# Four adaptive modulation units moved from TensorE's matmuls to multiply-and-add passes on VectorE

## What is computed

```python
mod = jax.nn.silu(c) @ w_ada[l] + b_ada[l]            # (1,1024) @ (1024, 6*1024)
shift1, scale1, gate1, shift2, scale2, gate2 = jnp.split(mod, N_MOD, axis=-1)
h  = modulate(rmsnorm(x, norm1_w[l]), shift1, scale1)
...
x  = x + gate1[:, None, :] * mix
h2 = modulate(rmsnorm(x, norm2_w[l]), shift2, scale2)
```

```python
t_mat = lax.linalg.triangular_solve(eye + a_mat, jnp.broadcast_to(eye, a_mat.shape),
                                    left_side=True, lower=True, unit_diagonal=True)
```

## Time and profile before

| | us |
|---|---|
| median of 3 runs (920.33 to 921.24) | 921.1 |
| the profiled execution | 920.74 |
| its span in the profile | 918.9 |
| TensorE busy | 894.8 (97%) |
| VectorE busy | 410.4 (45%) |
| ScalarE busy | 314.3 (34%) |
| GpSimd busy | 106.1 (12%) |

### The profile page before, as it was taken

One profiled execution on the slowest core, in us unless ns is written; L12 is line 12 of the kernel. 1 busy time (PEld: TensorE's weight loads), 2 busy tenths in 40 slices (PEclk: granted clock), 3 DMA queues, 4 the chain that ended last, 5 costly groups with the idle time before them and its releaser, 6 DMA issues.

```text
span 918.9 us, 13421 instructions
## 1 busy us (share of the span) xinstructions
PE 894.8 (97%) x5530; PEld 576.2 (63%) x5530; DVE 410.4 (45%) x697; ACT 314.3 (34%) x507; POOL 106.1 (12%) x116
## 2 busy tenths in 40 slices
PE   5999999999999999999999999999999999999998
PEld 2688876777644434444344444444435899999886
DVE  2457735368522323222222232223233878888744
ACT  1227435243522222232122212222213555555531
POOL 1024463131000000000000000000000022222200
PEclk9999999999999999999999999999999999999999
DMA  9962259787979999999999999999999665545301
GB/s 357 413 289 93 93 194 358 282 331 292 404 275 422 422 420 420 421 421 420 419 421 419 418 421 421 422 420 420 420 421 353 197 190 181 183 184 185 133 1 47
DMA packets 60892, 289.47 MB, mean 315 GB/s; under 512 B 4500, under 2 KB 28692, under 8 KB 33688
## 3 DMA queue, kind: packets, MB, share of 16 engines
q1 hardware_dynamic: 59104, 284.13, 78.0%
q10 hardware_dynamic: 1720, 4.40, 1.2%
HBM read 287.47 MB, written 1.05 MB: 314 GB/s over the span
## 4 chain that ended last, share of the span: by engine, by line
PE 91%; DVE 3%; DMA 2%; issue 2%; ACT 1%; POOL 1%; ACTq 0%; DVEq 0%
PE ps L1031 24%; PE ps L1055 12%; PE ps L536 8%; PE ps L1019 7%; PE ps L1152 7%; PE ps L1153 7%; PE ps L1154 7%; PE ps L619 4%; PE ps L1071 3%; PE ps L551 2%; PE ps L1044 2%; PE ps L519 2%; DMA S<-in_first_cols_dram 1%; DMA ring<-in_ada_units_dram 1%; PE ps L510 1%
## 5 line engine op out<-in xcount | busy, mean ns | idle before, releaser
L1034 PE MATMUL ps<-ring,proj 128*64 128x512 f32 x320 | 140.9, 593 | 0.0
L1031 PE MATMUL ps<-ring,proj 128*64 128x512 f32 x304 | 133.9, 593 | 0.0
L1852 DVE TENSOR_TENSOR w_l<-ring,w_h 128x2048 fp32r<-128x2048 f32 x33 | 75.5, 2291 | 44.8 <-ACT w_h L2200 44.8
L1152 PE MATMUL ps<-h_h,w_h 128*128 128x256 f32 x336 | 95.1, 283 | 0.0
L1153 PE MATMUL ps<-h_l,w_h 128*128 128x256 f32 x336 | 95.1, 283 | 0.0
L1154 PE MATMUL ps<-h_h,w_l 128*128 128x256 f32 x336 | 95.1, 283 | 0.0
L1031 PEld LDWEIGHTS ps<-ring,proj 128*64 128x64 f32 x304 | 41.1, 137 | 84.6 <-issue 84.6
L1708 DVE SCALAR_TENSOR_TENSOR RQ<-ps,gate_of,proj 128x512 f32<-128x512 f32 x32 | 24.0, 750 | 152.3 <-PE ps L1056 152.3
L1031 PE MATMUL ps<-arena,proj 128*64 128x512 f32 x208 | 91.6, 593 | 0.0
L2200 ACT CAST w_h<-ring 128x2048 fp32r<-128x2048 f32 x33 | 62.8, 1902 | 81.4 <-PE ps L1154 76.9
L2156 ACT CAST MX_r<-RQ 64x512 fp32r<-64x512 f32 x62 | 38.2, 616 | 145.8 <-DVE RQ L1708 145.0
(11 more groups left out here) (372 smaller groups left out, 1610.7 us busy)
## 6 DMA issues: line engine op xcount, KB each, us to landing
ring<-in_w_dram SPq DMA_DIRECT2D x114, 1024.0 KB, 16.4
arena<-in_w_dram SPq DMA_DIRECT2D x72, 1024.0 KB, 16.3
ring<-in_ada_units_dram SPq DMA_DIRECT2D x11, 2048.0 KB, 8.5
ring<-in_ffn_w_in_dram SPq DMA_DIRECT2D x22, 1024.0 KB, 7.8
ring<-in_in_units_dram SPq DMA_DIRECT2D x6, 2048.0 KB, 23.0
ring<-in_ffn_w_out_dram SPq DMA_DIRECT2D x5, 2048.0 KB, 8.0
arena<-in_in_units_dram SPq DMA_DIRECT2D x2, 2048.0 KB, 24.7
ring<-in_out_units_dram SPq DMA_DIRECT2D x2, 2048.0 KB, 9.1
```

What stands on the lines that cost most here:

```text
L1031: pe.matmul(ps[0:SLOTS, :], XTe[i % 2][:, k, :], u1[:, k, :], start=(k == 0), stop=(k == 7))
L1034: t = pe.matmul(ps[64:64 + SLOTS, :], XTe[i % 2][:, k, :], u3[:, k, :], start=(k == 0), stop=(k == 7))
L1152: pe.matmul(ps, ah, bh, start=first, stop=False)
L1852: ve.tensor_tensor(low, src, dst.bitcast(F32), ALU.subtract).then_inc(split_ready, 1)
```

## The change

Units 4 to 7 leave TensorE. VectorE makes them from the same loaded weights: a multiply of the first chunk with its column of silu(c) (`ccol`), one scalar for each partition, then seven multiply-and-adds, one for each further chunk, each waiting for the one before it. All 128 partitions now hold a part sum, so the totals multiply with `ones` instead of `sel`. Units 4 and 5 write to `part`, 6 and 7 write to (and read again from) the turned view of `by_eights`. VectorE's list has unit 4 at the end of level 1, unit 5 at the end of level 2, unit 6 in level 3 behind the row totals, unit 7 at the end of level 4. TensorE's `ada(4)` to `ada(7)` and ScalarE's four copies are gone; the row totals 4 and 5 move from level 4 to level 3, behind `project(5)`. The load that takes a unit's place waits for VectorE's last pass (`ada_rows`).

```diff
             def gate_total(j, src):
                 ps = take("total", j)
-                pe.wait_ge(*drained("ada", j))
-                pe.matmul(ps[:, :], sel, src, start=True, stop=True).then_inc(*mm.up("total", j))
+                pe.wait_ge(ada_rows, by_vector.index(j) + 1)
+                pe.matmul(ps[:, :], ones, src, start=True, stop=True).then_inc(*mm.up("total", j))
...
-                elif level == 5:
-                    ada(7)
                 elif level == 2:
                     project(3)
                 elif level == 3:
                     project(5)
-                elif level == 4:
                     gate_total(4, part[0])
                     gate_total(5, part[1])
+                elif level == 4:
                     turn_rotated(0)
...
                 elif level == 2:
                     project(4)
-                    ada(4)
-                elif level == 3:
-                    ada(5)
                 elif level == 4:
                     turn_rotated(1)
-                    ada(6)
...
+            def ada(j):
+
+                w = unit(("ada", j), 512)
+                if j in (4, 5):
+                    ve.wait_ge(*mm.of("columns", 1, 1))
+                    dst, cut = part[j % 2], lambda a: a
+                else:
+                    ve.wait_ge(*mm.of("total", 4))
+                    ve.wait_ge(*mm.of("total", 5))
+                    dst = by_eights[:, :, 64 * (j % 2):64 * (j % 2) + 64].rearrange("k c p -> k p c")
+                    cut = lambda a: a.rearrange("k (p c) -> k p c", c=8)
+                ve.wait_ge(*filled(("ada", j)))
+                ve.tensor_scalar(dst, cut(w[:, 0, :]), ccol[:, 0:1], None, ALU.mult).then_inc(*vd.up())
+                for c in range(1, 8):
+                    ve.wait_ge(*vd.now())
+                    ve.scalar_tensor_tensor(dst, cut(w[:, c, :]), ccol[:, c:c + 1], dst, ALU.mult,
+                                            ALU.add).then_inc(*((ada_rows, 1) if c == 7 else vd.up()))
...
                 if level == 1:
                     lower(3)
+                    ada(4)
                 elif level == 2:
                     lower(5)
+                    ada(5)
                 elif level == 3:
                     gate_total(4)
                     gate_total(5)
+                    ada(6)
+                elif level == 4:
+                    ada(7)
...
                 if kind == "ada":
-                    return mm.of("ada", i)
+                    return (ada_rows, by_vector.index(i) + 1) if i in by_vector else mm.of("ada", i)
```

More of the change, by code:

```diff
@@ L475, in program @@
         chunk_ready_a, chunk_ready_v = sem("chunk_ready_a"), sem("chunk_ready_v")
-        diagonal_ready = sem("diagonal_ready")
+        diagonal_ready, ada_rows = sem("diagonal_ready"), sem("ada_rows")
+        by_vector = (4, 5, 6, 7)
         rows_made, gated, router_scaled, h2_rows = (sem(n) for n in ("rows_made", "gated", "router_scaled", "h2_rows"))
@@ L556, in gate_total @@
                 ps = take("total", j)
-                pe.wait_ge(*drained("ada", j))
-                pe.matmul(ps[:, :], sel, src, start=True, stop=True).then_inc(*mm.up("total", j))
+                pe.wait_ge(ada_rows, by_vector.index(j) + 1)
+                pe.matmul(ps[:, :], ones, src, start=True, stop=True).then_inc(*mm.up("total", j))
             def column_total(seg, half, ps=None):
-                ps = ps or take("columns", seg)
-                pe.wait_ge(*drained("ada", 2 * seg + half))
+                ps, j = ps or take("columns", seg), 2 * seg + half
+                if j in by_vector:
+                    pe.wait_ge(ada_rows, by_vector.index(j) + 1)
+                else:
+                    pe.wait_ge(*drained("ada", j))
                 for c in range(8):
-                    i = pe.matmul(ps[64 * half:64 * half + 64, 2 * c:2 * c + 2],
-                                  by_eights[:, c, 64 * half:64 * half + 64], sel[:, 0:2], start=True, stop=True)
+                    i = pe.matmul(ps[64 * half:64 * half + 64, 2 * c:2 * c + 2], by_eights[:, c, 64 * half:64 * half + 64],
+                                  (ones if j in by_vector else sel)[:, 0:2], start=True, stop=True)
                 i.then_inc(*mm.up("columns", seg, half))
@@ L793, in tensor_program @@
                     ada(10)
-                else:
+                elif level == 6:
                     project(7)
@@ L1909, in ada @@
                 ps, dst = full("ada", j), part[j % 2]
[L1910 to L1914, removed]
+                if j in (8, 9):
+                    ac.wait_ge(*mm.of("columns", 3, 1))
                 elif j > 9:
                     dst = late_part[j % 2]
-                if j in (6, 7, 8, 9):
+                if j in (8, 9):
                     half = slice(64 * (j % 2), 64 * (j % 2) + 64)
```

## The result

The median after is 926.99 us (five runs, 925.49 to 928.67) against 921.1 before (919.5 to 921.66, five runs): a ratio of 1.0067, 95% interval 1.0050 to 1.0084, so 0.67% slower. The profiled execution took 928.67 us, with a span of 926.9; that of before 920.74 and 918.9.

The account below looks back on a forecast made before the run. TensorE, 91% of the chain that ended last, was taken as the bound: 7.4 us taken off, 18.7 put on, mostly waits behind units 6 and 7, so 11.5 us later, 932 us, range 922.5 to 943.

Parts of the forecast that it names:

- TensorE waits for it at the totals: At the level-3 row totals, TensorE would be held until unit 5 ends on VectorE at 135.2: 0.15 us.
- one turned pass: A VectorE multiply-and-add of units 6 and 7, writing and reading its target with a stride: 1.22 us, bounds 0.75 and 2.1.
- price of a collision, for a pass: A VectorE multiply-and-add meeting a GpSimd instruction of 0.72 us would alternate with it and pay about 0.6 us.
- TensorE until level 5 starts: TensorE would wait 11.4 us for the level-4 subtraction, which stands behind unit 6 in VectorE's queue.
- copy of the products, bare: The copy of the level-5 products, formerly hidden by unit 7 on TensorE, would be exposed: 0.7 us.
- wait for a bank before unit 10: TensorE's unit 10 would wait 4.5 us for a bank freed by VectorE's level-5 subtractions, queued behind unit 7.
- wait for the split: In the projection after level 6, TensorE would wait 1.6 us for VectorE's split after its first eight matmuls.
- rival 1: VectorE passes cost 0.78 us whatever the stride and GpSimd doesn't collide: 0.8 us gained, 920.3; chance 0.10.
- Rival 5: TensorE's clock falls in its waits, so sixteen uncovered projection matmuls run at half rate: up to 4 us more, 936; chance 0.12.
- Rival 3: On VectorE, stride paid but GpSimd collisions slight: 4.4 us less than the sum, 928; chance 0.16.
- rival 4: In units 6 and 7, strided reading and writing paid in turn, unit 16 us: twice 6.2 more, 945; chance 0.10.
- point of decision: A unit price of 6.4 us on VectorE decides the sign, since each microsecond of a turned unit counts twice.

Follow-up runs that it names:

- experiment 1: Against the changed kernel, units 6 and 7 went back to TensorE and ScalarE, only 4 and 5 stayed on VectorE: 916.53 us, ratio 0.9945 to before.
- experiment 2: Against the changed kernel, VectorE wrote units 6 and 7 in rows and TensorE took every eighth element when loading weights: 927.09 us, ratio 1.0064 to before.
- experiment 7: Against the changed kernel, GpSimd's eight multiplies that rotate the keys were left out (keys then wrong): 924.89 us, measured once.
- late7: Against the changed kernel, unit 7 moved behind VectorE's level-5 splits, and projection 4 loaded ahead of unit 9: 927.14 us, ratio 1.0060 to before.
- fill: Against the changed kernel, eleven matmuls that nothing reads were put into TensorE's wait ahead of level 5: 929.12 us, ratio 1.0075 to before.
- fill2: Against the changed kernel, unread matmuls in both TensorE waits, eleven ahead of level 5 and five ahead of its scores: 926.44 us, measured once.

## Why the prediction was right in direction and too large in size

Forecast 932.0 with 922.5 to 943, 10.9 over before; measured 927.0, 5.9 over. Slower had 0.90. By its own steps, forecast against measured:

| step | forecast | measured |
|---|---|---|
| unit 4 in rows, GpSimd idle | 6.0 us | 6.0 (0.47 + 5.48 and a step between) |
| unit 5, seven collisions | 10.2, end 135.2 | 9.0, end 133.7 |
| TensorE waits for it at the totals | 0.15 | none |
| one turned pass | 1.22 | 1.11 |
| price of a collision, for a pass | 0.6 | 0.36, plain or turned |
| GpSimd's last rotations start | 139.3 | 137.9 |
| collisions of unit 6 | 7 | 5, and 0.2 on its multiply |
| unit 6 | 14.1 | 10.4 |
| TensorE until level 5 starts | 11.4 | 6.41, and 0.94 for GpSimd's sum |
| copy of the products, bare | 0.7 | 0.94 |
| unit 7 | 9.9 | 8.7 |
| wait for a bank before unit 10 | 4.5 | none; half-rate work, 3.2, in its place |
| wait for the split | 1.6 | 0.67 |
| end of the stretch against before | +11.5 | +5.9 |
| behind it | passed on whole | passed on; 2.3 more in the profiled execution, not in the medians |

**What held.** The mechanism is the forecast one. The low price of units 4 and 5 held (experiment 1), the stride costs (experiment 2), GpSimd costs (experiment 7), level 4 and level 5 wait behind units 6 and 7 in VectorE's queue, and the loads cost nothing (no wait of TensorE for a transfer stands in the stretch). The rule of decision held too: TensorE's waits were to exceed 7.4 us for a slower kernel, and they are 9.4.

**The term that was mis-sized is the price of unit 6.** It was put at 9.9 + 4.2 = 14.1 us; it is 10.4, so 3.7 of the 5.6 that are missing stand there. Of these, 2.4 are the collisions (4.2 against the 1.8 of experiment 7), the rest the passes, which make unit 7 cheaper by the same 1.2. Two slips of the sum hardly matter: rival 1 counts from the median where the sum counts from the profiled execution (0.4 us), and GpSimd doesn't work on until 145 but is idle from 130.6 to 134.9. The collision was priced from one pair of long overlaps as if a pass waited for most of the other's 0.72 us. The line of all passes (duration min/median/max in ns), then one pass of unit 5 and one of unit 6 by themselves, each with the GpSimd instruction that it meets:

```profile
L1258 DVE SCALAR_TENSOR_TENSOR part<-ring,S,part x28: 752/1107/1460, 110.7 to 158.9; 128x512 f32<-128x512 f32 x28
```

```profile
126.83 1.10 DVE L1258 SCALAR_TENSOR_TENSOR part<-ring,S,part 128x512 f32<-128x512 f32 x1
...
141.88 1.46 DVE L1258 SCALAR_TENSOR_TENSOR part<-ring,S,part 128x512 f32<-128x512 f32 x1
```

```profile
126.21 1.18 POOL L2350 TENSOR_TENSOR S<-proj,S 128x256 f32<-128x256 f32 x1
...
137.87 3.05 POOL L2350 TENSOR_TENSOR S<-proj,S 128x256 f32<-128x256 f32 x4
...
141.00 1.43 POOL L2352 TENSOR_TENSOR proj<-S 128x256 f32<-128x256 f32 x1
```

A plain pass is 752 ns and 1.10 in company, a turned one 1107 and 1.46: about 0.36 us each time. The queues do alternate, as forecast (all seven passes of unit 5 take 1.10 to 1.12, the first five of unit 6 1.35 to 1.46), but half of each instruction goes by beside the other. Unit 6 meets only five because the last group of rotations starts at 137.87, not at 139.32 as before: the prediction had it start no earlier, but with unit 4 gone from TensorE the projection that it rotates comes 1.85 us earlier. Three of its four multiplies are over when unit 6 begins at 139.59, which leaves one multiply, two sums and two masks; they end at 146.9. GpSimd pays as well: its multiplies go from about 0.7 (2.78 for four) to 1.18 and its sums to 1.43, which is what TensorE's wait of 0.94 before the level-4 subtraction is for.

The Trainium skill's page SBUF — State Buffer, section Who interferes with whom, has the loser blocked for a whole instruction; here the trace doesn't bear that out for VectorE: by that rule a collision with a 0.72-us instruction would be 0.72, and it costs 0.36. For GpSimd beside a long VectorE instruction the trace agrees: its multiply at 122.71, beside the split that ends at 124.77, takes 2.67 us and ends 0.6 after it.

**The stride.** The pass was put at 1.22 between bounds of 0.75 and 2.1, on the choice that reading and writing don't add. That choice held: 1.11. The same page of the Trainium skill, section Door 1: The DMA port swizzle, lets each step to another 16-byte line pay, without a figure; the trace agrees with the direction, and the figure here is 0.36 us on 512 elements that are read and written so.

**The clock.** Rival 5 had 0 to 4 us, and I took 0: unit 7 on VectorE covers what follows the first wait, and the clock may rise before the projection's last sixteen matmuls. These ran at 1.00 (160 to 170 us in after), but the second wait, which was to lower the clock ahead of them, didn't come. As for the cover, late7 and fill show that the clock and unit 7 cover each other almost exactly, and fill2 that the stretch is no shorter with the clock at 2.4 GHz throughout. But the forecast had TensorE reach the bank early and wait 4.5 us there; it came late and slow instead. That this part of the sum has nearly its forecast size (3.2 + 0.67 against 4.5 + 1.6) is in part luck: the reason is one that it named only as a rival's.

**The chances.** Rival 3 (collisions slight, 928) came nearest in time, by 1 us, in part by luck: it had no collisions and dearer passes, and the two errors offset each other. Rival 1 and rival 4 fell with the first turned unit. The point of decision was given as 6.4 us for a unit. In rows beside GpSimd unit 6 took 7.9, and free of it unit 7 took 6.0; that kernel's stretch was still 2.6 longer than before, so for unit 6 it agrees. No run had both units under 6.4.

## What to carry to other kernels

Time that an engine idles before a link of the chain is room only up to its length: units 4 and 5 went into gaps of 5.9 and 12 us and gained 3.1, units 6 and 7 went into 1.3 and 6.1 us and lost 9.0, so price moved work against each gap, in the form and beside the neighbours it will have there, and move only what fits. Work on the bounding engine may be what fills its time while the chain passes through others; taking it away there buys waits. When two limits run side by side (here a queue and a clock), an experiment that lifts one alone shows nothing or a loss: lift both before either is ruled out.

## What the runs showed of the hardware that was not expected

- A multiply-and-add of 128x512 that writes its target with 512 bytes between neighbours, and reads it so too, takes 1107 ns; plain it takes 752. A copy that only writes so had cost as much more.
- A VectorE pass with two SBUF tensors loses 0.36 us to a GpSimd instruction of 0.72 us, whether the pass is 0.75 or 1.11 us long; the GpSimd instruction loses 0.46 to the short pass and 0.7 to 0.8 to the long one. The opening multiply, with one such tensor, loses too: 0.96 us instead of 0.47 in unit 5.
- Where 64-column weight loads take every eighth float, thirty-two matmuls of two columns with them last 3.55 us instead of 1.82.
- TensorE's granted clock fell from 2.4 to 1.2 GHz in a wait (after, 6.41 us), but also 1.2 us after a wait of 2.43 us was over (fill, at 162), and at the end of those thirty-two matmuls of two columns, in which TensorE was never idle. Before, the same count at 1.82 us had no such fall (the next unit takes 1.92 us).
- The same modulation unit at 18 us takes 1.92 us in some executions and 3.5 to 3.6 in others, of kernels that are the same up to there; this is most of the 1.8 us by which the start of the stretch varies.
